# Eight projection slabs beside the attention pairs in one seven-product form, and three ScalarE jobs moved in that stage

## The reference, cut to what matters

```
z = rms_norm(x) @ w_in                       # 256 x 1024 times 1024 x ...
z_lx, z_lg, q, k, v, f_logit, z_gates = split(z)
xr = causal_depthwise_conv(z_lx, width 4)
r, i = sigmoid(xr @ w_a + b_a), sigmoid(xr @ w_x + b_x)    # 8 blocks of 128
hr = scan(a, sqrt(-expm1(2 log_a)) * i * xr),  a = exp(-8 r softplus(-lam))
y_lru = (gelu(z_lg) * hr) @ w_lru_out
o = causal attention of 16 heads of 64, with forget-gate logits
m = sigmoid(gate_lru) * y_lru + sigmoid(gate_attn) * (o @ w_attn_out)
```

## Time and profile before

| | us |
|---|---|
| median of the runs shown | 2856.04 |
| the profiled execution's own time | 2856.47 |
| its span | 2854.3 |
| TensorE busy | 2423.1 (85%) |
| VectorE busy | 1144.8 (40%) |
| ScalarE busy | 508.8 (18%) |

### The profile page before, as it was taken

The page is one execution under the profiler, slowest core; times in us unless marked ns, Lnnn a source line. Parts: engine busy times, 40 slices in busy tenths (PEclk is TensorE's granted clock), DMA queues, the critical chain, the costliest instruction groups (busy, mean ns, idle before and its releaser), DMA issues.

```text
span 2854.3 us, 43608 instructions
## 1 busy us (share of the span) xinstructions
PE 2423.1 (85%) x19183; PEld 1856.3 (65%) x19183; DVE 1144.8 (40%) x2122; ACT 508.8 (18%) x1115; POOL 151.3 (5%) x274
## 2 busy tenths in 40 slices
PE   7989988665655666555999999999999999999999
PEld 4666774211211221112899877999999997789999
DVE  2555532000000000000655564775665556476655
ACT  4443421000000000000210125311011012451200
POOL 0364410000000000000000000000000000000000
PEclk9999988777778787787999999999999999999999
DMA  7544439999999999999545334344445444334543
GB/s 254 156 104 126 134 126 405 426 427 428 427 428 429 427 428 428 428 428 427 188 163 178 119 126 155 130 166 166 174 149 177 163 149 148 130 122 148 177 144 123
DMA packets 209225, 687.05 MB, mean 241 GB/s; under 512 B 36588, under 2 KB 73869, under 8 KB 183437
## 3 DMA queue, kind: packets, MB, share of 16 engines
q1 hardware_dynamic: 204685, 683.74, 62.1%
q10 hardware_dynamic: 4352, 0.53, 0.1%
HBM read 680.04 MB, written 4.19 MB: 240 GB/s over the span
## 4 chain that ended last, share of the span: by engine, by line
PE 61%; DMA 30%; DVE 3%; ACT 2%; POOL 1%; SPq 1%; issue 1%; ACTq 0%; DVEq 0%
PE bank L1861 17%; PE bank L1909 10%; DMA slab_ring<-in_moe_w_up 7%; DMA slab_ring_more<-in_moe_w_down 7%; DMA slab_ring_more<-in_moe_w_up 7%; DMA slab_ring<-in_moe_w_down 6%; PE bank L381 5%; PE bank L2042 4%; PE bank L2161 4%; PE bank L2093 3%; PE bank L1932 3%; PE bank L1374 3%; PE bank L1828 2%; DMA slab_ring_more<-in_moe_w_gate 1%; PE bank L1954 1%; PE bank L410 1%
## 5 line engine op out<-in xcount | busy, mean ns | idle before, releaser
L1374 PE MATMUL bank<-slab_ring,chosen_xT 128*32 128x512 f32 x1248 | 206.1, 798 | 123.0 <-DMA slab_ring<-in_moe_w_up 66.0
L1861 PE MATMUL bank<-slab_ring 128*128 128x128 f32 x2560 | 299.0, 275 | 0.4 <-ACT lru_gelu L2275 0.4
L1861 PEld LDWEIGHTS bank<-slab_ring 128*128 128x128 f32 x2560 | 292.3, 192 | 0.5 <-issue 0.5
L1531 DVE TENSOR_TENSOR beaten_then_hidden<-bank,beaten_then_hidden 128x512 f32<-128x512 f32 x16 | 11.1, 691 | 557.9 <-PE bank L1374 557.9
L1861 PE MATMUL bank<-layer_uT,slab_ring 128*128 128x128 f32 x1920 | 227.5, 275 | 0.0
L1861 PEld LDWEIGHTS bank<-layer_uT,slab_ring 128*128 128x128 f32 x1920 | 221.1, 192 | 0.2
L1374 PEld LDWEIGHTS bank<-slab_ring,chosen_xT 128*32 128x32 f32 x1248 | 39.5, 128 | 276.8 <-DMA slab_ring<-in_moe_w_up 110.0
L1374 PE MATMUL bank<-slab_ring_more,chosen_xT 128*32 128x512 f32 x800 | 132.8, 799 | 91.5 <-DMA slab_ring_more<-in_moe_w_up 47.3
L1909 PE MATMUL bank<-slab_ring 128*128 128x128 f32 x1408 | 165.7, 275 | 0.0
L1909 PEld LDWEIGHTS bank<-slab_ring 128*128 128x128 f32 x1408 | 161.4, 192 | 0.0
L1374 PEld LDWEIGHTS bank<-slab_ring_more,chosen_xT 128*32 128x32 f32 x800 | 25.4, 130 | 194.5 <-DMA slab_ring_more<-in_moe_w_up 79.0
(11 more groups left out here) (456 smaller groups left out, 3673.9 us busy)
## 6 DMA issues: line engine op xcount, KB each, us to landing
slab_ring<-in_w_up SPq DMA_DIRECT2D x44, 2048.0 KB, 8.0
slab_ring<-in_moe_w_up SPq DMA_DIRECT2D x39, 2048.0 KB, 46.3
slab_ring<-in_moe_w_gate SPq DMA_DIRECT2D x39, 2048.0 KB, 45.3
slab_ring<-in_moe_w_down SPq DMA_DIRECT2D x38, 2048.0 KB, 46.1
slab_ring<-in_w_in SPq DMA_DIRECT2D x28, 2048.0 KB, 8.0
slab_ring_more<-in_moe_w_down SPq DMA_DIRECT2D x26, 2048.0 KB, 46.6
slab_ring_more<-in_moe_w_gate SPq DMA_DIRECT2D x25, 2048.0 KB, 45.3
slab_ring_more<-in_moe_w_up SPq DMA_DIRECT2D x25, 2048.0 KB, 45.8
```

The lines of the kernel that those rows point to most:

```text
L1374: ins = nc.tensor.matmul(out[32 * c:32 * c + 32, 0:cols], x, slot_of((q * EXPERT_SLABS + i) % NRE).rearrange("p (k n) -> p k n", k=2 if co ...
L1861: i = nc.tensor.matmul(out[:, j * P:(j + 1) * P], a[:, k, j * P:(j + 1) * P], x[:, k, :], start=(start and j == 0 and k == 0), stop=(k == ...
```

## The change

All eight slabs beside the attention pairs go through one function `mix_slab(u)`, u = 0 to 7, in the seven-product form. Its body for u of 4 and up is that of `gate_slab`. The results of slabs 0 and 1 (z_lx) go to the SBUF tile `r`, those of 2 and 3 (z_lg) to `gl`, those of 4 to 7 to `gates` as before. `lx_out` and `taps` then read `r`, and `lg_out` works in place in `gl`, where they read PSUM before. `scores(u)` now stands ahead of the wait for the slab. Step 8 keeps the plain form. The tile addresses, banks and semaphore counts change with it.

```diff
+    MIX_BANKS = ((0, 1, 2), (3, 1, 2))
+    MIX_SLAB = (24, 25, 26, 29, 30, 31, 32, 33)
+    def mix_quarter(u, i, t):
+        tile, first = ((r, 0), (gl, 2), (gates, 4))[u // 2 if u < 4 else 2]
...
-            with_pair(0, uT, "lx_ps", (0, 1), wait_v(0))
-            with_pair(1, uT, "lx_ps", (2, 3), wait_v(1))
-            with_pair(2, uT, "lg_ps", (0, 1), wait_n("xr", 0))
+            def mix_slab(u):
+                scores(u)
+                w = take().rearrange("p (k n) -> p k n", k=KC)
...
+                else:
+                    joined(u - 2, J_21)
+                if u == 3:
+                    pe.wait_ge(ly.sem["i"], ly.value(l, "i", 2))
+                product(X, w[:, 0:4, 0:256], uT[:, 0:4, 0:P], start=True).then_inc(ly.next("up_ps"), 1)
+                if u:
+                    joined(u - 1, J_12)
+                if u == 3:
+                    pe.wait_ge(ly.sem["i"], ly.value(l, "i", 4))
+                summed(1)
+                product(Y, S1, T1, start=True).then_inc(ly.next("up_ps"), 1)
+                if u:
+                    probs_transposed(u - 1, 0)
+                summed(2)
+                copied(K_P1)
+                product(X, S2, T2).then_inc(ly.next("up_ps"), 1)
...
+                if u:
+                    heads_out(u - 1)
+                joined(u, J_22)
+                used(product(X, w[:, 4:8, 256:512], T4))
+            mix_slab(0)
+            mix_slab(1)
+            mix_slab(2)
...
-            with_pair(3, uT, "lg_ps", (2, 3), wait_n("i", 0))
-            for v in range(4):
-                gate_slab(v)
+            for u in range(3, 8):
+                mix_slab(u)
```

ScalarE's list:

```diff
-            exps(0)
-            lx_out(0)
...
-            for step in range(4, 8):
-                if step > 4:
-                    gate_out(step - 5)
-                if step == 5:
-                    decay_root()
-                gate_copied(step - 4, 0)
...
+            for u in range(8):
+                if u in (1, 2):
+                    lx_out(2 * u - 2)
+                    lx_out(2 * u - 1)
+                mix_copied(u, 0)
+                exps(u)
+                mix_copied(u, 2)
+                if u:
+                    probs_out(u - 1, 0)
+                mix_copied(u, 1)
+                if u:
+                    probs_out(u - 1, 1)
+                if u == 3:
+                    decay_rates()
+                elif u == 4:
+                    decay_tanh()
+                    for b in range(4):
+                        lg_out(b)
+                elif u == 5:
+                    decay_root()
+                if u > 4:
+                    gate_out(u - 5)
+                if u:
+                    heads_out(u - 1)
+                if u == 2:
+                    rx_out(0)
+                    rx_out(1)
```

VectorE's list (`mix_wsums(0, True)` and `mix_wsums(0, False)` are also placed between the joins of the second v slab):

```diff
+            mix_wsums(0, True)
             v_joined(1, 0, 0, W_P2, K_P1, 2, 0)
+            mix_wsums(0, False)
             v_joined(1, 1, 1, W_P7, K_P5, 0, 2)
...
+            for u in range(8):
+                masked(u)
+                if u in (1, 2):
+                    taps(2 * u - 2)
+                if u == 3:
+                    mix_wsums(3, False)
+                elif u == 7:
+                    lru(2)
+                elif u != 2:
+                    mix_wsums(u + 1, True)
+                normed(u)
+                mix_joined(u, 0, 0, W_P2, K_P1, 2, 0)
+                if u == 2:
+                    taps(3)
+                elif u < 7:
+                    mix_wsums(u + 1, u == 3)
+                mix_joined(u, 1, 1, W_P7, K_P5, 0, 2)
+                if u == 1:
+                    taps(1)
+                elif u > 4:
+                    lru((0, 1, 3)[u - 5])
+                mix_joined(u, 0, 1, W_P3, K_U2, 1, 1)
+                if u == 3:
+                    mix_wsums(4, False)
+                mix_joined(u, 1, 0, None, None, 0, None)
+                if u == 2:
+                    ig_products()
+                    mix_wsums(3, True)
```

More of the change, by code:

```diff
@@ L2025, in heads_out, with last_pair_beside @@
                 i.then_inc(ly.next("o_ps"), 1)
-            def with_pair(step, x, name, banks, before):
+            def last_pair_beside(x, before):
                 w = take()
-                if step < 8:
-                    scores(step)
                 for j in range(4):
@@ L2189, in tail_slab @@
                 used(product(X, w[:, 4:8, 256:512], T4))
-            pe.wait_ge(ly.sem["joined"], ly.value(l, "joined", g_joined_at(3, J_21)))
+            pe.wait_ge(ly.sem["joined"], ly.value(l, "joined", mix_joined_at(7, J_21)))
             pe.wait_ge(ly.sem["s_masked"], ly.value(l, "s_masked", 8))
@@ L2807, in vector @@
             dve.wait_ge(ly.sem["cumt"], ly.value(l, "cumt", 1))
-            masked(0)
-            normed(0)
-            taps(0)
-            taps(1)
-            masked(1)
-            normed(1)
-            taps(2)
-            taps(3)
-            masked(2)
-            normed(2)
-            for c in range(4):
-                dve.wait_ge(ly.sem["i"], ly.value(l, "i", c + 1))
-                if c == 3:
-                    dve.wait_ge(env.slab_free, through(l, S_WX))
-                nc.vector.tensor_tensor(ig[:, 2 * c:2 * c + 2, :], ig[:, 2 * c:2 * c + 2, :], xr[:, 2 * c:2 * c + 2, :], ALU.mult).then_inc(ly.next("ix"), 1)
@@ L2841, in g_joined @@
-            def g_joined(v, i, t, made, copied, bank, own):
-                dst = gates[:, 4 * v + 2 * i:4 * v + 2 * i + 2, t * P:(t + 1) * P]
-                src = two(ps[G_BANKS[v][bank]][:, 0:T])
-                if own is None:
-                    dve.wait_ge(env.slab_free, through(l, S_G + v))
-                    ins = nc.vector.tensor_copy(dst, src)
-                else:
-                    dve.wait_ge(ly.sem["up_ps"], ly.value(l, "up_ps", g_up_at(v, made)))
-                    dve.wait_ge(ly.sem["up_copy"], ly.value(l, "up_copy", g_copied_at(v, copied)))
-                    ins = nc.vector.tensor_tensor(dst, src, tail_kept[v % 2][own], ALU.add)
-                ins.then_inc(ly.next("joined"), 1)
@@ L2854, in vector, with ig_products @@
-            masked(3)
-            normed(3)
-            g_wsums(0, True)
-            g_wsums(0, False)
-            for v in range(4):
-                masked(4 + v)
-                if v < 3:
-                    g_wsums(v + 1, True)
-                else:
-                    lru(2)
-                normed(4 + v)
-                g_joined(v, 0, 0, W_P2, K_P1, 2, 0)
-                if v < 3:
-                    g_wsums(v + 1, False)
-                g_joined(v, 1, 1, W_P7, K_P5, 0, 2)
-                if v:
-                    lru((0, 0, 1, 3)[v])
-                g_joined(v, 0, 1, W_P3, K_U2, 1, 1)
-                g_joined(v, 1, 0, None, None, 0, None)
+            def ig_products():
+                for c in range(4):
+                    dve.wait_ge(ly.sem["i"], ly.value(l, "i", c + 1))
+                    if c == 3:
+                        dve.wait_ge(env.slab_free, through(l, S_WX))
+                    nc.vector.tensor_tensor(ig[:, 2 * c:2 * c + 2, :], ig[:, 2 * c:2 * c + 2, :], xr[:, 2 * c:2 * c + 2, :], ALU.mult).then_inc(ly.next("ix"), 1)
```

237 lines of the change are left out of this document (98 added, 139 removed).

## The result

| | before | changed |
|---|---|---|
| runs compared, median us | 2856.57 (2855.12 to 2858.28, 4 runs) | 2834.54 (2832.27 to 2835.88, 4 runs) |
| ratio, 95% interval | | 0.9923 [0.9911, 0.9935] |
| profiled execution, its span | 2856.47, 2854.3 | 2832.27, 2830.4 |

The changed kernel is 22.0 us faster, where 20.5 was forecast against the median shown. First comes the stage. Here is a table of stretches of the changed kernel, first layer: the steps 0, 1 and 2, then the four small slabs, then steps 3 to 6. The columns are those of the earlier trace rows.

The account below looks back on a forecast made before the run. TensorE's own work was taken as the bound in the two layers' half. Gains of 10.1 and 11.5 us, together 21.6, less 0.7 for the clock, gave 20.9 off 2856.47; forecast 2835.5 us, range 2831 to 2846.

Parts of the forecast that it names:

- D: Rival, chance 0.05: late VectorE, late slab 29 and later pushes leave no gain; 2859 us, within noise of before.
- the clock: Second layer, step 5: the clock's part of the gain, 1.45 us, taken at half, so 0.7 off the sum.
- The form, steps 0 to 2: Seven-product form in steps 0 to 2 saves TensorE 1.32, 1.32 and 1.23 us per layer.
- rival C: Chance 0.03: 128-wide products not bound by columns, steps 0 to 2 stay as long; 7.7 us less gain, 2843.2.
- J_22 of step 1: VectorE's join that the seventh product awaits: ready at 13.95 us, needed at 14.08, so no wait.
- Rival A: Chance 0.12: VectorE becomes the bound of steps 0 to 3, only waits go; gain 10.6 us, 2845.5.
- six taps from SBUF: VectorE, steps 1 and 2: between 2.2 and 4.3 us, taken as 2.68; the dearest add 2.5 us per layer.
- Step 3: Falls to 16.30 us, with a new 0.24 us wait for a probability copy; gains 3.31 and 3.23 us by layer.
- Slab 29: Step 3: its 8.01 us transfer lands at 1.1 us, hidden behind scores running to 1.71; 1.2 us wait gone.
- Rival B: Chance 0.05: slab 29 late, its transfer taking 13 us; step 3 grows by 4.4 us in both layers, 2844.
- Step 5 and the root: ScalarE's root and gate sigmoids follow the second probability copy; step 5 falls to 16.06 us, gaining 2.91 and 4.36 by layer.
- Rival E: Chance 0.03: VectorE 2.5 us late in each of steps 0 to 3, clock falling behind each wait; 32 us more, 2867.

Follow-up runs that it names:

- two additions in step 1: Changed kernel with two unused 128x512 VectorE additions ahead of the join J_22 in step 1 of each layer; 2834.65 us, ratio 0.992.
- form alone: Changed kernel with root and gate sigmoids put back at the step's start, ahead of the copy of the first partial product; 2840.38 us, ratio 0.9948.
- slab's wait first: Changed kernel with the wait for the slab put back ahead of `scores(u)`, as in the kernel before; 2841.43 us, ratio 0.9943.
- six additions: Changed kernel with six unused 128x512 VectorE additions ahead of the join J_22 in step 1 of each layer; 2850.77 us, ratio 0.9976.

## Why the prediction was right

**Total.** 2835.5 was predicted and 2834.54 measured, and with no wait left in the stage D, in which nothing is left over, falls at once. The stage gives 22.24 us in the two traces against a sum of 21.6; the 0.6 more lie in step 3 with the small slabs ahead of it (3.58 and 3.51 for 3.31 and 3.23) and in step 2. From the sum 0.7 was taken for the clock, whose part (1.45) came in full in the executions compared. So the gain was forecast 1.5 us too small, 20.5 for 22.0, and that the two times are only 1.0 apart is partly luck: the median of the kernel before came out 0.5 higher with its fourth run. By the prediction's own working (2856.47 - 20.9 - 0.4) the time would have been 2835.2 and not 2835.5.

**The form, steps 0 to 2.** Predicted 14.40, 16.06, 16.06; measured 14.41, 16.06, 15.97. Step 2 is 0.09 shorter than step 1, as it was before (17.29 against 17.38); the prediction gave that back without a reason, and its -1.23 is -1.32. The form is worth the same in all three steps. Two views show why: one group of 16 records of 256 columns before, with the start of what follows it, and the same of 128 columns after.

```profile
1700.24 3.62 PE L2042 MATMUL bank<-layer_uT,slab_ring 128*128 128x256 f32 x16
1703.69 0.49 PE L2012 MATMUL bank<-const_masks,ffn_hidden 128*128 128x128 f32 x3
```

```profile
2462.86 1.95 PE L2071 MATMUL bank<-layer_uT,slab_ring 128*128 128x128 f32 x16
2464.64 0.49 PE L2019 MATMUL bank<-const_masks,ffn_hidden 128*128 128x128 f32 x3
```

Taken from the starts, 16 records of 256 columns are 3.45 us, 216 ns each, and 16 of 128 columns are 1.78, 111 ns each. Then 64 x 0.216 = 13.8 and 112 x 0.111 = 12.4, which leaves 1.4 us, about the 1.32 of the step. Halving the columns nearly halves the time, and rival C falls. The Trainium skill's rule, "TensorE: Matmul & The Clock Gate", Back-to-back issue gap (81 ns at 128 columns, 131 at 512, weight load included), is not what these float32 records show: they take 111 ns at 128 columns and 216 at 256, both dearer than its figures, and halving the columns gives 0.51 of the time.

**VectorE's slack.** Predicted: J_22 of step 1 at 13.95 for 14.08. These are VectorE and TensorE there, in the timeline of the changed kernel:

```profile
1696.07 2.69 DVE L2785 SCALAR_TENSOR_TENSOR lru_x<-lru_r,layer_vecs_all,lru_x 128x253 f32<-128x253 f32 x6
...
1703.69 1.22 DVE L2758 TENSOR_TENSOR slab_ring<-slab_ring 128x1024 f32<-128x1024 f32 x1
1704.82 0.41 DVE L2769 TENSOR_TENSOR lru_r<-bank,slab_ring 128x256 f32<-128x256 f32 x1
1705.77 2.05 PE L2071 MATMUL bank<-slab_ring 128*128 128x128 f32 x16
```

The join ends at 1705.23 and the product starts at 1705.77, 14.08 after the step's start as predicted; J_22 is there 0.54 ahead, not 0.13. The prediction had added up durations where neighbours overlap by up to 0.09 us. The two additions in step 1 find the same slack: 1.44 put in, 0.9 of it waited for. Rival A, VectorE as the bound, was thus half a microsecond away in step 1, and no more than that. The unknown of the sum, six taps from SBUF between 2.2 and 4.3 us, is 2.69, where 2.68 was taken.

**Step 3.** Predicted 16.30 with a new wait of 0.24; measured 16.10 and 16.09. ScalarE's copy, the second transpose and `decay_rates` there:

```profile
1739.41 0.47 ACT L2369 ACTIVATE probsT<-bank 128x384 f32<-128x384 f32 x1
1740.00 0.49 PE L2019 MATMUL bank<-const_masks,ffn_hidden 128*128 128x128 f32 x3
1740.92 3.29 ACT L2420 ACTIVATE lru_x<-lru_r,lru_softplus 128x256 f32<-128x256 f32 x8
```

The transpose starts 9.28 after the step's start, which is just when it was wanted. The copy ahead of it ends at 9.16 and not at 9.4, since the exponentials started at 6.65 and not at 6.85: again a sum of rounded pieces that was a little too long. The term of 0.24 was thus all but nothing (0.04 in the step), with nothing to spare: the transpose starts 0.12 behind the end of the copy. `decay_rates` behind the copies delays nobody. That its place alone ends the old 0.9 us wait is argued and not shown, since every kernel here with the new place also has the new form.

Slab 29 is the other half. It is hidden in the trace compared, as predicted, and its room is what the prediction made it: the transfer starts 6.8 us ahead of the step and the product wants it 1.71 in, which is 8.5 us (the prediction: 8.01, and 0.6 more until 1.7). What the prediction didn't have is how much the transfer varies. In the twelve profiled executions it took 7.7 to 9.7 us, and where it took more than 8.5 the excess shows as a wait (9.05 gave 0.5, and 9.55 in the form alone gave 1.0). In the kernels with `scores` ahead of the slab's wait that happened in 9 of 18 layers, at 0.4 to 1.2 us each. Rival B had asked for a transfer of 13 us, which none of them showed; a small form of it comes at 9 us.

**Step 5 and the root.** The jobs stand where they were predicted. ScalarE's queue, with the first `lru` operation of VectorE:

```profile
1773.20 1.28 ACT L2432 ACT_TABLE_LOAD   x1
1774.49 1.91 ACT L2432 ACTIVATE lru_r<-lru_r 128x2048 f32<-128x2048 f32 x1
1776.42 1.28 ACT L2411 ACT_TABLE_LOAD   x1
1776.51 0.69 DVE L2821 SCALAR_TENSOR_TENSOR lru_r<-lru_x,lru_r 128x512 f32<-128x512 f32 x1 [1.12 <-ACT lru_r L2432]
1777.72 1.71 ACT L2411 ACTIVATE ffn_hidden<-ffn_hidden,layer_vecs_all 128x256 f32<-128x256 f32 x4
1779.33 0.36 ACT L2374 ACTIVATE qnT<-bank 128x256 f32<-128x256 f32 x1
```

Times from the step's start at 1762.88: load 10.3, root's end 13.5, `lru(0)` 13.6, heads' copy out at 16.8, against the forecast 10.3, 13.5, 13.5, 16.9. The root starts 1.29 behind its load's start. VectorE's last operation ahead of the masking of step 6 ends at 17.75, where 17.6 was predicted and 17.89 is wanted.

The Trainium skill's drain behind a table load, "ScalarE: Activation LUTs", What ACT_TABLE_LOAD costs, is not there for either of the loads shown: the activations start 1.29 and 1.30 behind the start of their loads, and the second load starts 0.02 behind the end of the root. What the prediction made of such a drain, a masking of step 6 that is 1.1 late and 2 us lost by it, isn't borne out either: with the gate sigmoids ahead of the root the masking was 2.8 late and made no wait of its own.

**The clock.** Rival E said that a fall comes with 2.5 us of wait and none below it. The first half was right in its direction and the bound was wrong: of three waits of 2.0 (form alone, slab's wait first) two are followed by a fall, and of two of 2.5 one is. Its price per fall, 1.45, is the least that was seen: form alone paid 1.45 again, slab's wait first 3.2, and the six additions some 1.7 in one layer (5.2 + 0.3 less the wait) and 6.0 in the other (5.6 + 4.2 less the wait). The price goes with how long the clock stays at its lower level: 3.4, 3.4, 6.9, 3.4 and 13.6 us in these five cases, in this order, and a little under half of that is lost. What makes it stay longer isn't shown. That changes nothing for the forecast, since no wait of this size was left, but E would have had to be counted from about 2.0 us of lateness a step and not from 2.5. Step 1 is 0.5 plus 2.0 of added VectorE work away from it.

Not tried: the taps at another price, since they can't be made dearer alone without a changed step, and the changed kernel with slab 29 asked for earlier, which needs another slot.

## What to carry to other kernels

Price a step by an undisturbed neighbour that already has the new form, and then follow the other engines' queues to the instant at which the first engine wants each result: here that gave every step within 0.2 us. A job on a helper engine costs nothing in the gap between its last timely delivery and the next; in front of a delivery it costs what it makes that delivery late by (6.2 us of loads, root and sigmoids ahead of the copy made TensorE wait 2.0 and 2.5 us). A wait of TensorE of 2 us or more can cost more than its length: in 5 of 7 such waits here the clock fell, and in one of them it stayed low until 9 us into the next step.

## What the runs showed of the hardware that was not expected

- The same transfer of 2 MB (slab 29, same place in the order) took between 7.7 and 9.7 us over the twelve profiled executions, over 8.8 in 7 of them in the second layer and in 3 in the first, and never between 8.1 and 8.8. A margin that covers the value of one trace is not a margin.
- The lower clock follows some waits of 2.0 to 2.5 us and not others, in kernels with the same instructions around them: 2.5 fell in layer 2 and not in layer 1 (before), 2.0 fell in layer 1 and not in layer 2 (form alone). Waits of up to 1.2 were never followed by one in this stage. With 3.8 us both fell, for 13.6 us in one layer and 3.4 in the other.
- For `lx_out` it matters that the source is now SBUF: two activations of 128x256 take 1.09 us, and took 1.02 from PSUM. For VectorE's taps it does not: 2.69 and 2.68 for six. The rows of `lx_out` are those of the changed kernel and of the one before:

```profile
1692.26 1.09 ACT L2381 ACTIVATE lru_x<-lru_r,layer_vecs_all 128x256 f32<-128x256 f32 x2 [0.70 <-DVE lru_r L2765]
```

```profile
1703.89 1.02 ACT L2378 ACTIVATE lru_x<-bank,layer_vecs_all 128x256 f32<-128x256 f32 x2 [0.59 <-PE bank L2042]
```
